# A mixture-of-experts loop on one core: final layer norm moved from behind the loop into it, experts e and e+16 paired

## The reference, cut to what matters

```python
def layer_norm(x, g, b):
    mu = jnp.mean(xf, -1, keepdims=True)
    var = jnp.mean(jnp.square(xf - mu), -1, keepdims=True)
    return ((xf - mu) * lax.rsqrt(var + EPS) * g + b).astype(x.dtype)

def hier_moe(u, ...):
    g_idx = jnp.argmax(g_logits, axis=-1)
    e_in = jnp.einsum('ng,nge->ne', jax.nn.one_hot(g_idx, N_GROUPS), e_logits)
    top_v, top_i = lax.top_k(e_in, TOP_K)                  # two experts of one group
    e_glob = g_idx[:, None] * EXP_PER_GROUP + top_i
    for e in range(N_EXPERTS):                             # 32 experts, 1024 -> 256 -> 1024
        he = jax.nn.silu(t @ w_g[e]) * (t @ w_u[e])
        y = y + combine[:, e:e + 1] * (he @ w_d[e])

hp = layer_norm(DN_ALPHA * hp + ff, ln2_g[l], ln2_b[l])    # the final normalisation, 512 rows
hs = layer_norm(DN_ALPHA * hs + ff, ln2_g[l], ln2_b[l])    # and 64 rows
```

## Time and profile before

| | us |
|---|---|
| median of 3 runs (lowest, highest) | 955.1 (954.59, 956.13) |
| the profiled execution | 962.32 |
| its span, first to last instruction | 960.5 |
| TensorE busy in the span | 841.3 (88%) |
| VectorE, ScalarE, GpSimd busy | 393.6, 263.0, 73.9 |

### The profile page before, as it was taken

How to read it: one execution, slowest core, us unless ns; L and a number is a source line. 1 busy time by engine, 2 the same in 40 slices (tenths; PEclk the granted TensorE clock), 3 DMA queues, 4 the chain that set the end, 5 groups by cost and what they waited for, 6 DMA issues and landing times.

```text
span 960.5 us, 12457 instructions
## 1 busy us (share of the span) xinstructions
PE 841.3 (88%) x5174; PEld 623.3 (65%) x5174; DVE 393.6 (41%) x776; ACT 263.0 (27%) x521; POOL 73.9 (8%) x96
## 2 busy tenths in 40 slices
PE   2799999998999999999999999994999888787750
PEld 2789999885788778899999984543533333232220
DVE  4445653668635555732314034438122212111118
ACT  6266111344424345522122200001111101011113
POOL 1200400000000000000000010000111100100010
PEclk9999999999699999999999999995799989898975
DMA  9221643101113342222223078309499999999726
GB/s 323 90 88 45 197 127 93 45 2 44 45 50 113 119 132 72 86 69 88 67 88 96 19 283 351 139 23 394 153 419 416 418 420 417 421 419 419 321 95 236
DMA packets 65367, 178.70 MB, mean 186 GB/s; under 512 B 7168, under 2 KB 41184, under 8 KB 52880
## 3 DMA queue, kind: packets, MB, share of 16 engines
q1 hardware_dynamic: 53792, 144.45, 40.1%
q0 software_dynamic: 10832, 31.04, 9.1%
q10 hardware_dynamic: 688, 2.43, 0.7%
HBM read 165.33 MB, written 21.36 MB: 194 GB/s over the span
## 4 chain that ended last, share of the span: by engine, by line
PE 69%; SPq 9%; DMA 9%; DVE 8%; ACT 3%; issue 1%; ACTq 0%; POOLq 0%; DVEq 0%
PE bank L1605 14%; PE bank L1606 13%; PE bank L1607 13%; PE bank L1897 7%; SPq L548 7%; PE bank L1974 6%; DMA wgu<-in_w_exp_up 6%; SPq L552 2%; PE bank L1996 2%; PE bank L1813 1%; PE bank L1713 1%; DVE ring L1092 1%; PE bank L1961 1%; PE bank L1833 1%; PE bank L1842 1%
## 5 line engine op out<-in xcount | busy, mean ns | idle before, releaser
L1605 PE MATMUL bank<-hT,ring 128*128 128x288 f32 (+2 forms) x608 | 185.3, 305 | 14.9 <-DVE ring L1092 12.9
L1607 PE MATMUL bank<-hT,ring 128*128 128x288 f32 (+2 forms) x608 | 182.7, 300 | 0.0
L1974 PE MATMUL bank<-wgu,XT 128*64 128x512 f32 x512 | 130.2, 667 | 35.8 <-DMA wgu<-in_w_exp_up 34.2
L1605 PEld LDWEIGHTS bank<-hT,ring 128*128 128x128 f32 (+1 forms) x608 | 115.8, 190 | 21.4 <-DVE ring L1092 13.7
L1974 PEld LDWEIGHTS bank<-wgu,XT 128*64 128x64 f32 x512 | 44.0, 153 | 120.0 <-issue 111.3
L1607 PEld LDWEIGHTS bank<-hT,ring 128*128 128x128 f32 (+1 forms) x608 | 116.0, 191 | 0.6
L1092 DVE TENSOR_TENSOR ring<-ring,ring 128x2048 fp32r<-128x2048 f32 (+2 forms) x32 | 68.0, 2126 | 96.7 <-ACT ring L779 96.6
L779 ACT ACTIVATE ring<-ring 128x2048 fp32r<-128x2048 f32 (+2 forms) x32 | 56.1, 1752 | 112.6 <-PE bank L1607 112.3
L1897 PE MATMUL bank<-ring,osb 128*128 128x512 f32 (+1 forms) x160 | 70.2, 594 | 1.0 <-DVE osb L1358 1.0
L1606 PE MATMUL bank<-hlo_r,ring 128*128 128x288 f32 x240 | 70.7, 295 | 0.0
L1537 DVE TENSOR_TENSOR act<-bank,sil 128x256 f32<-128x256 f32 x16 | 6.8, 425 | 154.8 <-PE bank L1982 136.7
(11 more groups left out here) (337 smaller groups left out, 1395.0 us busy)
## 6 DMA issues: line engine op xcount, KB each, us to landing
wgu<-in_w_exp_gate SPq DMA_DIRECT2D x32, 1024.0 KB, 22.2
wgu<-in_w_exp_up SPq DMA_DIRECT2D x32, 1024.0 KB, 23.8
wd<-in_w_exp_down SPq DMA_DIRECT2D x32, 1024.0 KB, 25.1
ring<-in_w_in SPq DMA_DIRECT2D x17, 1024.0 KB, 5.2
ring<-in_w_in SPq DMA_DIRECT2D x8, 512.0 KB, 4.7
s<-in_state_gla POOLq DMA_DIRECT2D x4, 1024.0 KB, 6.0
out<-s POOLq DMA_DIRECT2D x4, 1024.0 KB, 5.1
ring<-in_w_gla_br SPq DMA_DIRECT2D x4, 1024.0 KB, 5.1
```

What stands on the lines that cost most here:

```text
L1605: pe.matmul(out, sh, mh, start=first, stop=False)
L1607: return pe.matmul(out, sl, mh, start=False, stop=last)
L1974: ins = pe.matmul(bk[t, :].rearrange("p (h f) -> p h f", h=2), XT[:, kc, t], wgu[n][a][:, :, kc, :], start=(kc == 0), stop=(kc == KC - 1))
```

## The change

The final normalisation goes into the loop, at the pair that holds a token's second expert (the later of its two in the order of pairs). `y_d` shrinks to one row for each token and is filled with the inputs early in the program, so that every row holds something; `send` scatters only the rows whose token meets its first expert in this pair (the others get row number 4096). New on GpSimd: `previous(g+1)` gathers into `Pv` the first results of the tokens whose second expert is in pair g+1, and `finish(g)` scatters the normalised rows from `Ut` to the two output tensors, in two DMAs, one that skips sample rows and one that skips prompt rows. VectorE gets `finished(g)`, ScalarE `squares(g)`. The read-back, the five tiles and the stores behind the loop are gone.

Experts e and e+16 make a pair instead of 2e and 2e+1, so that a token's two experts, which lie in one group of eight, are never in one pair. Overflow beyond 64 tokens would now take a whole pair for one expert; with these inputs there is none, before or after.

```diff
             def expert(g, a):
-                return slice(2 * g + a, 2 * g + a + 1)
+                return slice(g + 16 * a, g + 16 * a + 1)
...
+            pool.dma_start(y_d[0:SEQ, :], A["x_prompt"][0]).then_inc(y_set, 16)
+            pool.dma_start(y_d[SEQ:TQ, :], A["x_sample"].rearrange("b t d -> (b t) d")).then_inc(y_set, 16)
...
+            def previous(g, rows):
+
+                n, k = y_place(g - 1) if isinstance(g, int) else (FIXED % NY, g + (FIXED // NY - FIXED - 1))
+                pool.wait_ge(y_sent[n], k * 16 + 16)
+                hold(g)
+                if not isinstance(g, int) or g > 1:
+                    pool.wait_ge(z_sq, g - 1)
+                    hold(g)
+                    pool.wait_ge(u_done, g - 1)
+                    hold(g)
+                pool.indirect_dma_start(out=Pv, out_offset=None, in_=y_d[:, :],
+                                        in_offset=bass.IndirectOffsetOnAxis(ap=rows, axis=0),
+                                        bounds_check=TQ - 1, oob_is_err=False).then_inc(prev_in, 16)
+
+            def finish(g, prompt, sample):
+
+                pool.wait_ge(z_ready, g)
+                hold(g)
+                pool.indirect_dma_start(out=O[0][0], out_offset=bass.IndirectOffsetOnAxis(ap=prompt, axis=0), in_=Ut,
+                                        in_offset=None, bounds_check=SEQ - 1, oob_is_err=False).then_inc(rows_out, 16)
+                pool.indirect_dma_start(out=O[1].rearrange("b t d -> (b t) d"),
+                                        out_offset=bass.IndirectOffsetOnAxis(ap=sample, axis=0), in_=Ut,
+                                        in_offset=None, bounds_check=NS - 1, oob_is_err=False).then_inc(rows_out, 16)
...
                 send(g, tbi[:, 1, g:g + 1])
                 if g + NX <= FIXED:
                     gather(g + NX, tbi[:, 0, g + NX:g + NX + 1])
+                if g == 0:
+                    pool.wait_ge(finish_ready, 1)
+                previous(g + 1, tbi[:, 2, g + 1:g + 2])
+                if g:
+                    finish(g, tbi[:, 2, g:g + 1], tbi[:, 3, g:g + 1])
...
+            def squares(g):
+
+                step(act.activation(epsc[:, 1:2], epsc[:, 0:1], ACT.Sqrt), g, 1)
+                act.wait_ge(z_sum, g)
+                for x in range(2):
+                    step(act.activation(last_bank[:, :], Pv[:, 512 * x:512 * x + 512], ACT.Square, bias=z_stat[:, 0:1],
+                                        accum_out=z_stat[:, 1 + x:2 + x]), g, 2 + x)
+                step(act.activation(z_stat[:, 4:5], z_stat[:, 1:2], ACT.Identity, scale=1.0 / D, bias=epsc[:, 0:1]), g, 4)
+                act.activation(z_stat[:, 5:6], z_stat[:, 2:3], ACT.Sqrt, scale=1.0 / D, bias=z_stat[:, 4:5]).then_inc(z_sq, 1)
+                step(act.activation(epsc[:, 1:2], epsc[:, 0:1], ACT.Silu), g, 5)
...
+            def finished(g):
+
+                dve.wait_ge(prev_in, g * 16)
+                dve.wait_ge(y_rows, g + 1)
+                dve.scalar_tensor_tensor(Pv, Pv, 1.0, Yt[:, y_place(g)[0], :], ALU.mult, ALU.add,
+                                         accum_out=z_stat[:, 3:4]).then_inc(z_added, 1)
+                dve.wait_ge(z_added, g)
+                dve.tensor_scalar(z_stat[:, 0:1], z_stat[:, 3:4], -1.0 / D, None, ALU.mult).then_inc(z_sum, 1)
+                if not isinstance(g, int) or g > 1:
+                    dve.wait_ge(rows_out, g * 32 - 32)
+                dve.wait_ge(z_sum, g)
+                dve.scalar_tensor_tensor(Ut, Pv, z_stat[:, 0:1], lng, ALU.add, ALU.mult).then_inc(u_done, 1)
+                dve.wait_ge(z_sq, g)
+                dve.reciprocal(z_stat[:, 6:7], z_stat[:, 5:6]).then_inc(z_rstd, 1)
+                dve.wait_ge(z_rstd, g)
+                dve.wait_ge(u_done, g)
+                dve.scalar_tensor_tensor(Ut, Ut, z_stat[:, 6:7], lnb, ALU.mult, ALU.add).then_inc(z_ready, 1)
```

More of the change, by code:

```diff
@@ L343, in decoder_kernel @@
         h1_d = nc.dram_tensor("h1_rows", [TQ, D], f32, kind="Internal").ap()
-        y_d = nc.dram_tensor("expert_rows", [2 * TQ, D], f32, kind="Internal").ap()
+        y_d = nc.dram_tensor("first_rows", [TQ, D], f32, kind="Internal").ap()
         w2_in = sem("w2_in")
@@ L423, in decoder_kernel @@
         y_rows = sem("y_rows")
-        y_back = [sem(f"y_back{i}") for i in range(TILES)]
-        y_out = sem("y_out")
         out_done = sem("out_done")
-        y_ready = sem("y_ready")
-        loop_done = sem("loop_done")
+        finish_ready = sem("finish_ready")
+        prev_in = sem("prev_in")
+        z_sum, z_step, z_sq, z_ready, u_done = sem("z_sum"), sem("z_step"), sem("z_sq"), sem("z_ready"), sem("u_done")
+        z_added, z_rstd, rows_out = sem("z_added"), sem("z_rstd"), sem("rows_out")
         OUTS = [0]
@@ L600, in _ @@
                 pair_down_in(g, both)
-            sp.wait_ge(loop_done, 1)
-            for i in range(TILES):
-                r = ROWS[i]
-                sp.dma_start(y0[0:r, i, :], y_d[i * P:i * P + r, :]).then_inc(y_back[i], 16)
-                sp.dma_start(y1[0:r, i, :], y_d[TQ + i * P:TQ + i * P + r, :]).then_inc(y_back[i], 16)
-            for i in range(TILES):
-                sp.wait_ge(y_ready, i + 1)
-                dst = O[0][0, i * P:i * P + P, :] if i < 4 else O[1].rearrange("b t d -> (b t) d")
-                sp.dma_start(dst, y0[0:ROWS[i], i, :]).then_inc(y_out, 16)
-            sp.wait_ge(y_out, 16 * TILES)
         @block.gpsimd
@@ L1019, in _ @@
                     drain_xt(g + 2)
+                if g:
+                    squares(g)
             act.wait_ge(list_ready, 1)
@@ L1024, in _ @@
                 drain_at(g)
+                squares(g)
                 drain_xt(g + 1)
-            link(act.activation(epsc[:, 1:2], epsc[:, 0:1], ACT.Sqrt))
-            for i in range(TILES):
-                r = ROWS[i]
-                act.wait_ge(y_sum, i + 1)
-                link(act.activation(junk2[0:r, :], y0[0:r, i, :], ACT.Square, bias=mv[0:r, i, 0:1],
-                                    accum_out=mv[0:r, i, 1:2]))
-                act.activation(rstd[0:r, i:i + 1], mv[0:r, i, 1:2], ACT.Sqrt, scale=1.0 / D, bias=epsc[0:r, 0:1])\
-                   .then_inc(y_sq, 1)
         @block.vector
@@ L1491, in pair_values @@
                 return dve.tensor_tensor(onepair[:, :, n, :], hot, ten(R["val"][:, 10 * n:10 * n + 10], COLS), ALU.mult)
-            for n in range(2):
-                pair_values(n).then_inc(hot_ready, 1)
+            pair_values(0).then_inc(hot_ready, 1)
+            for k in range(2):
+                ins = dve.tensor_tensor(R["e10"][:, 5 * k:5 * k + 5], R["pair"][:, 5 * k:5 * k + 5],
+                                        R["pair"][:, 5 - 5 * k:10 - 5 * k], ALU.is_lt)
+            link(ins)
+            link(dve.tensor_tensor(R["val"][:, 10:20], R["val"][:, 0:10], R["e10"], ALU.mult))
+            pair_values(1).then_inc(hot_ready, 1)
             for n in range(2):
@@ L1552, in _ @@
             drain_xt(1)
+            dve.wait_ge(ln_in, 96)
             for g in range(FIXED):
@@ L2065, in constants @@
     put("restart", np.tile(np.arange(5 * N_EXP) % 5 != 0, (P, 1)) * 1.0)
-    put("vals", np.concatenate([tok, tok, tok, tok + TQ], axis=1) - float(PAD_ROW))
+    put("vals", np.concatenate([tok, tok], axis=1) - float(PAD_ROW))
     put("iota", np.tile(np.arange(P), (P, 1)))
-    put("pid", p[:, None] - N_EXP)
-    put("plow", np.where(p < N_EXP, p, 0)[:, None])
-    put("evens", np.tile(2.0 * np.arange(9), (P, 1)))
-    put("eid", np.tile(64 * np.arange(N_EXP), (P, 1)))
-    put("e31", np.tile(64 * (31 - np.arange(N_EXP)), (P, 1)))
+    put("pid", np.where(p < N_EXP, -1, (p - N_EXP) // 2)[:, None])
+    put("plow", np.where(p < N_EXP, p // 2 + 16 * (p % 2), 0)[:, None])
+    first = P * (np.arange(N_EXP) % 16) + 64 * (np.arange(N_EXP) // 16)
+    put("eid", np.tile(first, (P, 1)))
+    put("e31", np.tile(P * 16 - 64 - first, (P, 1)))
     return c
```

83 lines of the change are left out of this document (40 added, 43 removed).

## The result

| | before | changed |
|---|---|---|
| median (lowest, highest), us | 955.6 (954.59, 962.32), 4 runs | 971.2 (967.49, 972.97), 4 runs |
| the profiled execution, us; its span | 962.32; 960.5 | 972.97; 971.1 |
| start of gate and up of pair 15 | 911.31 | 936.33 |
| pair 15's result done | 926.82 | 951.99 |
| from there to the end of the span | 33.7 | 19.1 |

The ratio of the times is 1.0144 (95% interval 1.0119 to 1.0168): slower, by 15.6 us on the medians and by 10.6 us between the two profiled executions. The profiled execution of before lies 6.7 us above its median, that of the changed kernel 1.8 us above its own. I come back to that 5 us under the third experiment.

The account below looks back on a forecast made before the run. Bound before: expert weights through the DMA engines; after: GpSimd's chain of transfers. Pair 15's result at 926.8 + 25.6 = 952.4, plus 10.5 gives 962.9 against 960.5; 957.5 us on the median, 8-in-10 range 940 to 974.

Parts of the forecast that it names:

- The chain: GpSimd's queue: send landing, fetch, two stores, next send in line set the pair's time and delay pair 15 by 25.6 us.
- Pitch: Time from one fetch on GpSimd to the next: 17.4 us, from 5.0 before the first turn, 11.4 for four transfers, 0.8.
- Rival A: Expert loop: the weight stream stays the bound, with 16.1 us or less between fetches; 942.9 us on the median; chance 0.27.
- rival B: GpSimd's queue: a longer chain, 18.6 us between fetches; 970.7 us on the median; chance 0.22.
- Rival C: Expert loop: transfers land as fast as behind it, 2.2 to 4.3 us, so no chain binds; 943 us; chance 0.04.
- Pair 15's start: Gate and up of pair 15 on TensorE starts at 936.9 us, 25.6 us after 911.3, behind down of pair 14.
- The end: Behind pair 15's result: sums, normalisation, two stores and landing take 10.5 us in place of 33.7, a gain of 23.2 us.
- Router and pairing: Router ahead of the loop: three small operations and wider tables delay the tables, and all of the loop, by 1.0 us.
- Bytes in the stream: DMA in the loop: 576 more rows, 5.6 us, and skipped-slot packets, 4.4 us, end the weights 10 us later.
- Hidden work: VectorE's 4.4 and ScalarE's 5.5 us a pair lie in their waits, except the SiLU load at pair 13.
- The difference carried to the median: The trace difference, 962.9 against 960.5, was assumed the same on the median of 955.1, giving 957.5 us.
- the forecast's own 950 to 966: Median time range if the chain of about 17.4 us sets the pace; chance 0.47.

Follow-up runs that it names:

- experiment 3: Kernel before, with GpSimd ending its program only after the last output rows are stored: 961.4 us, ratio 1.0059.
- experiment 1: Changed kernel, with the fetch reading rows of h1 and GpSimd not waiting for the previous pair's send to land: 960.8 us, ratio 1.0049.
- experiment 2: Changed kernel without the second of each pair's two stores, the one to the sample rows: 957.2 us, ratio 1.0002.
- experiment 12: Kernel before, with two more transfers, all rows skipped, on GpSimd's queue ahead of the send of each of pairs 0 to 14: 966.5 us, ratio 1.0103.
- experiment 6: Kernel before, with only the changed kernel's pairing (experts e and e + 16) and its tables: 961.2 us, ratio 1.0053.
- experiment 10: Changed kernel with normalisation one pair later, and the fetch for pair g issued ahead of its send: 966.2 us, ratio 1.0094.
- experiment 4: Changed kernel with SiLU in place of both square roots per pair, so ScalarE's two table loads fall away: 969.4 us, ratio 1.0125.
- experiment 5: Changed kernel, with the two stores issued ahead of the next pair's fetch on GpSimd, pairs 1 to 13: 991.4 us, ratio 1.0364.
- experiment 9: Changed kernel with the whole normalisation one pair later, the fetch issued behind send and gather: 993.8 us, ratio 1.0399.
- experiment 7: Changed kernel, with the wait for the last stores' landing moved from GpSimd to VectorE: 969.3 us, ratio 1.0126.
- experiment 8: Changed kernel, with stores ahead of the next fetch (pairs 1 to 13) and the last wait moved to VectorE: 987.3 us, ratio 1.0313.

## Why the prediction was right in its direction, and where it was not

**The chain.** Right in size, and in mechanism for GpSimd's queue; that a second way through VectorE, ScalarE and down is about as long, it did not say. Pitch 17.4 us forecast, 17.62 measured. Its parts: 2.85 us a transfer from packet turns (11.4 / 4); measured, fetch to send is three places and (3.94 + 12.8 - 7.9) / 3 = 2.9 us, and 5.0 us (7.9 - 2.9) pass before the first turn. Rival A would have needed 16.1, rival B 18.6. Experiments 1 and 2 show it as the cause, by cutting the wait and by taking out one transfer, and experiment 12 closes such a ring in the kernel before. Behind the stream, with no weights to take turns with, the last two stores land 2.7 us after their issue. The turn-by-turn reading is also a rule of the Trainium skill (DMA: Bandwidth & Descriptors, "SWDGE vs HWDGE vs iDMA"): the queues of the two kinds are separate inside a DMA engine, and it serves them round-robin; the 2.9 us agree with it.

What the pitch costs is another matter. Starts of gate and up, from TensorE's timeline (us):

```
pair                   3        7       14       15
experiment 3       713.2    763.9    885.3    906.4
changed            714.1    780.8    905.6    936.3
```

From pair 7 to 14 the changed kernel takes 17.8 us a pair, the kernel before 17.3: there the weights had set much the same pace. Of the 30 us by which pair 15 is late, 16 arise between pairs 3 and 7, where the weights lay ready and a pair had taken 11.8 us, and 9.6 at the last step, where down of pair 14 waits for the squares.

**Rival C** is excluded for the loop: sends land in 12.8 us, not in 2 to 4. The stores behind the stream land in 2.7.

**Pair 15's start.** 936.9 forecast, 936.33 measured, but that is luck: errors cancel twice on the way. The fetch for pair 13 goes at 920.14, as forecast (919.9), because pair 2's went 2.2 us earlier than in the sum (726.35, not 728.5) and the pitch is 0.2 us longer. The rows of pair 13 then land 3.3 us earlier than I took (924.1 against 927.4, since the weights were through by then), and down of pair 14 takes 6.56 us instead of the 3.65 of the earlier trace rows. TensorE ran it at a granted clock of 0.55, near the lower of its two levels (1.2 of 2.4 GHz), after a stretch in which it had been busy 0.33 of 10 us:

```profile
920.00:930.00 10.00, 0.33 (x4) 0.14 (x5) 5.07 (x8) 4.19 (x10) 5.19 (x5) 0.61 0.19 60
930.00:936.50 6.50, 6.50 (x18) 1.92 (x20) 0.75 (x1) 1.39 (x2) 2.36 (x3) 0.55 0.32 92
```

(window, its length, busy time of TensorE, its weight loads, VectorE, ScalarE and GpSimd with instruction counts, granted clock, DMA share, GB/s; profile after.)

**The end: the step that failed.** "Sum 10.5 us in place of 33.7: a gain of 23.2 us." The sums, stores and landing came out 0.6 us longer: 951.99 to 963.08 is 11.1 us. What I left out is that GpSimd's program then has to close, 7.83 us that lie open. The gain is 14.6 us, and the end came at 971.1 instead of 962.9. Experiment 3 shows the same step in the kernel before, 5.6 us for 5.05. The Trainium skill (VectorE: DVE Perf Modes, "The DRAIN you can't avoid") tells of DRAINs of about 12 ns on all five engines, which come from the runtime's preamble and postamble. The DRAIN here bears a line of the kernel and takes 5.05 to 7.83 us on GpSimd, so that figure does not price it.

**Router and pairing.** For the tables 1.0 us was forecast. From the first sums of the router on TensorE to gate and up of pair 0 it is 20.8 us in the changed kernel and 19.2 before, so 1.6 us, of which experiment 6 has 1.24. That the pairing costs no more was never argued; alone it costs about 5 us, the tables among them.

**Bytes in the stream.** 10 us forecast; hidden in the changed kernel, where the weights do not bind. Where they bind again it shows: pair 14 starts at 895.0 in experiment 10 and 896.6 in 1, against 888.2 with the pairing alone: 7 to 8 us.

**Hidden work.** VectorE's and ScalarE's work is hidden but for ScalarE at some pairs, not at pair 13 alone as I wrote: the chain of work passes through its table load at 726, 758, 864, 897, 928 and 941 us. Experiment 4 prices its table loads at about 2 us in all.

**The difference carried to the median.** I assumed 2.4 us for both. The profiled execution of before was some 5 us slower in its loop than a usual one, so the same trace difference is larger on the medians. With that, the time of 971.2 us lies above the forecast's own 950 to 966 and next to rival B's 970.7, which is luck for B: its longer pitch of 18.6 us did not come. The closing step and those 5 us make the difference from 957.5.

Together, against the execution of experiment 3: 32.0 us late at the last result, 21.8 us gained behind it (32.9 from result to the last landing, 11.1 now), 7.8 us closing step: 18.0 us. The spans differ by 17.9 us, 971.1 less the 958.2 of experiment 3 without its 5.05. How much of the 32.0 us is the pairing's, no run separates.

## What to carry to other kernels

Work that leaves a tail has to be priced where it goes: here each pair took three more transfers on a queue whose first landing was already awaited, and 2.9 us a place is what counted, not the 4.4 and 5.5 us of engine work, most of which was hidden. A ring as long as the stream that already bounds the loop cost little where that stream bound it (17.8 us a pair for 17.3), and much where the loop had run ahead. Before reordering such a loop, write out each ring (issue, landing, consumer, next issue, buffer by buffer): two of my orders (experiments 5 and 9) removed one wait and closed a longer ring, 20 and 23 us slower than the changed kernel, and one swap of two issues gave 27.6 us back. And look at what each engine has still to do after its last useful instruction before you let it finish last.

## What the hardware showed that I had not expected

A transfer lands later for every transfer ahead of it in GpSimd's queue, whether its rows move or are skipped; rows that move add to it (the gather lands 15.3 + 1.3 - 12.8 = 3.8 us behind the send ahead of it). Issue to landing inside the stream of weights, by place in the pair's burst (issues are 1.3 us apart, 1.9 behind the fetch in experiment 10 and 1.8 behind the send in 9; two stores, and the two skipped transfers, share one median):

```
                      first        second        third         later
before                send 8.4     gather 10.9
changed               fetch 7.9    stores 10.1                 send 12.8, gather 15.3
12, two skipped       skipped 8.2 (both)         send 11.5     gather 13.5
9, one pair later     send 8.7     gather 10.3   fetch 12.1    stores 14.0
10, fetch ahead       fetch 9.4    send 10.9     gather 13.4   stores 14.4
```

GpSimd's closing step grows with what its queue carried: 5.05 us before and with the pairing alone, 6.52 with 30 skipped transfers more, 6.60 with one store a pair, 7.75 to 7.83 in all programs with the changed kernel's transfers (counted from the last store's issue in experiments 7 and 8). It does not depend on when they went: it is 5.05 in the kernel before and in experiments 3 and 6, and 7.83 in the changed kernel and in 1, 4 and 5, whose spans lie between 958.4 and 986.6 us. One store fewer in each of 15 pairs took 1.23 us from it, 0.08 us a transfer. No run here hid it where GpSimd stored last.
